# A two-block transformer kernel: column groups in the compressed products, the last steps by row tile, and three reorderings

## What is computed

```python
def compress_kv(kv, pe, w1, b1, w2):        # 15 windows of 32 rows, stride 16, for 2 groups
    blocks = kv[:, idx] + pe[None, None, :, None, :]
    flat = blocks.transpose(0, 1, 3, 2, 4).reshape(B, n_cmp, G, CMP_BLOCK * dk)
    hid = jax.nn.gelu(flat @ w1 + b1)       # a sum over 32 positions of 128 x 128 products
    return hid @ w2
...
    o_cmp = jnp.einsum('bghqn,bngd->bqghd', p.astype(v_cmp.dtype), v_cmp)
    o = gc[..., 0:1] * o_cmp + gc[..., 1:2] * o_slc + gc[..., 2:3] * o_win
...
    x = x + rms_norm(u @ w_down[l], norm_mlp_post[l])     # the end of the program
```

## Time and profile before

| | us |
|---|---|
| median of 3 runs | 2525.02 |
| the profiled execution | 2525.11 |
| its span | 2523.3 |
| PE busy (matmuls) | 2499.6, 99% of the span |
| PEld busy (weight loads) | 2111.9 |
| DVE busy | 1519.8 |
| ACT busy | 1223.3 |
| POOL busy | 47.9 |

### The profile page before, as it was taken

One profiled execution on the slowest core, in us unless ns is written; L12 is line 12 of the kernel. 1 busy time (PEld: TensorE's weight loads), 2 busy tenths in 40 slices (PEclk: granted clock), 3 DMA queues, 4 the chain that ended last, 5 costly groups with the idle time before them and its releaser, 6 DMA issues.

```text
span 2523.3 us, 32700 instructions
## 1 busy us (share of the span) xinstructions
PE 2499.6 (99%) x12440; PEld 2111.9 (84%) x12440; DVE 1519.8 (60%) x1766; ACT 1223.3 (48%) x1555; POOL 47.9 (2%) x67
## 2 busy tenths in 40 slices
PE   9999999999999999999999999999999999999998
PEld 7888888888888888888887887788788888888886
DVE  5656655655776567746764347655665565564565
ACT  6444556545655355534554444445544443443443
POOL 0101100000000000000000000000000000000000
PEclk9999999999999999999999999999999999999999
DMA  8665455655655555555557455555466556565663
GB/s 318 198 192 173 161 167 164 229 184 167 203 193 190 194 190 184 195 189 194 188 184 241 135 184 164 159 167 183 150 202 192 191 186 198 188 195 188 193 204 117
DMA packets 253216, 472.48 MB, mean 187 GB/s; under 512 B 23296, under 2 KB 28928, under 8 KB 252464
## 3 DMA queue, kind: packets, MB, share of 16 engines
q1 hardware_dynamic: 253104, 470.95, 57.3%
HBM read 468.78 MB, written 2.13 MB: 187 GB/s over the span
## 4 chain that ended last, share of the span: by engine, by line
PE 98%; DVE 1%; issue 1%; ACT 0%; DMA 0%; POOL 0%; POOLq 0%; SPq 0%; DVEq 0%; ACTq 0%
PE psum L1793 22%; PE psum L1759 20%; PE psum L1761 20%; PE psum L1760 19%; PE psum L1798 12%; PE psum L1894 1%; PE psum L1879 1%; PE psum L1820 1%; PE psum L2064 1%; PE psum L1864 1%; PE psum L1854 0%; DVE x_rows L1627 0%; PE psum L2153 0%; PE psum L2016 0%; PE psum L2141 0%
## 5 line engine op out<-in xcount | busy, mean ns | idle before, releaser
L1156 DVE TENSOR_TENSOR wl<-raw,wh 128x1024 fp32r<-128x1024 f32 x855 | 1048.0, 1227 | 930.0 <-ACT wh L713 924.9
L713 ACT ACTIVATE wh<-raw 128x1024 fp32r<-128x1024 f32 x855 | 904.7, 1060 | 1018.1 <-PE psum L1761 607.1
L1759 PE MATMUL psum<-wh,ha 128*128 128x512 f32 x1728 | 692.5, 401 | 0.4 <-DVE ha L1198 0.4
L1761 PE MATMUL psum<-wh,ha 128*128 128x512 f32 x1728 | 674.5, 390 | 0.0
L1760 PE MATMUL psum<-wl,ha 128*128 128x512 f32 x1728 | 672.8, 389 | 0.0
L1761 PEld LDWEIGHTS psum<-wh,ha 128*128 128x128 f32 x1728 | 324.3, 188 | 69.7
L1759 PEld LDWEIGHTS psum<-wh,ha 128*128 128x128 f32 x1728 | 324.7, 188 | 65.8 <-issue 0.8
L1760 PEld LDWEIGHTS psum<-wl,ha 128*128 128x128 f32 x1728 | 325.0, 188 | 65.1
L1793 PE MATMUL psum<-ha,wh 128*128 128x512 f32 x1408 | 336.6, 391 | 0.0
L1793 PEld LDWEIGHTS psum<-ha,wh 128*128 128x128 f32 x1408 | 258.7, 188 | 50.0
L1793 PE MATMUL psum<-hb,wh 128*128 128x512 f32 x1024 | 246.5, 392 | 0.0
(11 more groups left out here) (227 smaller groups left out, 1235.2 us busy)
## 6 DMA issues: line engine op xcount, KB each, us to landing
raw<-in_w_up SPq DMA_DIRECT2D x152, 1024.0 KB, 5.1
raw<-in_w_in SPq DMA_DIRECT2D x116, 1024.0 KB, 5.1
raw<-in_w_down SPq DMA_DIRECT2D x108, 1024.0 KB, 5.0
raw<-in_w_out SPq DMA_DIRECT2D x32, 1024.0 KB, 4.9
raw<-in_w_branch_a SPq DMA_DIRECT2D x8, 1024.0 KB, 4.9
raw<-in_w_branch_b SPq DMA_DIRECT2D x8, 1024.0 KB, 5.0
raw<-in_w_in SPq DMA_DIRECT2D x7, 512.0 KB, 8.3
x_t<-in_x_t SPq DMA_DIRECT2D x8, 256.0 KB, 7.7
```

Source lines behind the costliest of these rows:

```text
L713: act.activation(wh[q % SPLIT_SLOTS][:], raw[q // 2 % RAW_SLOTS][:, 2 * (q % 2):2 * (q % 2) + 2, :], ACT.Copy).then_inc(hi_done, 1)
L1156: dve.tensor_tensor(wl[q % SPLIT_SLOTS][:], raw[q // 2 % RAW_SLOTS][:, 2 * (q % 2):2 * (q % 2) + 2, :], wh[q % SPLIT_SLOTS][:].bitcast(F32 ...
L1759: pe.matmul(acc, hi, wh[s][:, c, :], start=first and c == 0, stop=False)
L1761: ins = pe.matmul(acc, lo, wh[s][:, c, :], start=False, stop=last and c == 1)
```

## The change

- Compressed products: each l goes to one of four groups of 32 PSUM partitions (l modulo 4), with 32 stationary columns (two of them zero), all 32 products of a kv in one piece after steps 15 and 17. The four partial sums are copied as 128 partitions, and the transposes after step 20 become products with `fold`, four stacked identities, which add them up. DVE builds fold and the zero columns at step 11.
- cmp_v and cmp_pt get 128 partitions; POOL zeroes them, and L1891 takes all 128.
- In the last block, steps 4 to 7 are done for row tile 0 first and then for tile 1. Sum, squares, mean, root, additions and output go by tile, with a root for each.
- The memset of warm comes ahead of the wait for par; par's DMA comes first.
- In the retention loop the division of the probabilities (j = 3) comes ahead of the split on DVE; the wait for rtab_in moves to the first rotation; the second pair of plain_lo goes from j == 5 to 4.

```diff
+CMP_M = 32
+CMP_GROUPS = P // CMP_M
-    cmp_in = at("cmp_in", [P, 2, CMP_BLOCK, 2, NCMP], 198)
+    cmp_in = at("cmp_in", [P, 2, CMP_BLOCK, CMP_M], 198)
-    cmp_v = at("cmp_v", [NCMP, 2, HD], 188)
+    cmp_v = at("cmp_v", [P, 2, HD], 188)
-    cmp_pt = at("cmp_pt", [NCMP, 8, SEQ], 180)
+    cmp_pt = at("cmp_pt", [P, 8, SEQ], 180)
...
# SP
+        sp.dma_start(par[:, 0:Q_BQ], a["params"][:, 0:Q_BQ]).then_inc(sem["par_in"], 16)
         x_piece(0)
         sp.dma_start(raw[0][:, 0, :], w_in[:, 0, 0:COLS]).then_inc(sem["raw_k0"], 16)
-        sp.dma_start(par[:, 0:Q_BQ], a["params"][:, 0:Q_BQ]).then_inc(sem["par_in"], 16)
...
+        sp.wait_ge(sem["post_ok"], 8 + 3)
+        sp.dma_start(o[:, 0, 0:3 * COLS], x_rows[:, 0, 0:3 * COLS]).then_inc(sem["out_in"], 16)
+        sp.wait_ge(sem["post_ok"], 8 + 4)
+        sp.dma_start(o[:, 0, 3 * COLS:], x_rows[:, 0, 3 * COLS:]).then_inc(sem["out_in"], 16)
+        for c in range(4):
             cols = slice(c * COLS, (c + 1) * COLS)
+            sp.wait_ge(sem["post_ok"], 12 + c + 1)
+            sp.dma_start(o[:, 1, cols], x_rows[:, 1, cols]).then_inc(sem["out_in"], 16)
# POOL
+        pool.wait_ge(sem["gate_ok"], 1)
+        pool.memset(cmp_v[:], 0.0).then_inc(sem["cmp_clear"], 1)
+        pool.wait_ge(sem["cin_ok"], 2)
+        pool.wait_ge(sem["cs_mm"], 1)
+        pool.memset(cmp_pt[:], 0.0).then_inc(sem["cmp_clear"], 1)
...
-        late_root(5, 2)
+        late_root(5, 2, (0,))
+        late_root(5, 3, (1,))
# DVE
+        dve.memset(warm[:], 0.0).then_inc(sem["warm_set"], 1)
         dve.wait_ge(sem["par_in"], 16)
...
+            if s == 11:
+                by = ident[:].rearrange("p (g m) -> p g m", g=CMP_GROUPS)
+                chain.link(dve.tensor_tensor(fold[:], by[:, 0, :], by[:, 1, :], ALU.add))
+                for g in range(2, CMP_GROUPS):
+                    chain.link(dve.tensor_tensor(fold[:], fold[:], by[:, g, :], ALU.add))
+                dve.memset(cmp_in[:, :, :, 2 * NCMP:CMP_M], 0.0)
...
-        dve.wait_ge(sem["rtab_in"], 48)
         for s in range(8 * RET_BLOCKS):
+            scaled = s < RET_START and s % SLOT == 2
+            if scaled:
+                head_stage(3, N1 + s // SLOT, NH)
             ahead(S_RET + s)
-            if s < RET_START:
+            if s < RET_START and not scaled:
                 head_stage(1 + s % SLOT, N1 + s // SLOT, NH)
             if s in rotations:
+                if rotations[s] == (0, 0):
+                    dve.wait_ge(sem["rtab_in"], 48)
...
-            if j in (2, 5):
-                for f in range(2 * (j == 5), 2 * (j == 5) + 2):
+            if j in (2, 4):
+                for f in range(2 * (j == 4), 2 * (j == 4) + 2):
...
+        last_columns(0)
+        tile_mean_square(0)
+        dve.wait_ge(sem["norm_rs"], 6)
+        for c in range(3):
+            add_normed(5, slice(c * COLS, (c + 1) * COLS), (0,))
+        last_columns(1)
+        add_last(0)
+        tile_mean_square(1)
+        dve.wait_ge(sem["norm_rs"], 7)
+        for c in range(3):
+            add_normed(5, slice(c * COLS, (c + 1) * COLS), (1,))
+        add_last(1)
# TensorE
+        def tile_by_tile(q0, src, g, ready):
+            for t in range(NT):
+                acc = psum[:, row_bank(g) + t, :]
+                for j in range(4, 8):
+                    if t == 0:
+                        ready(j)
+                        pe.wait_ge(lo_done, q0 + j + 1)
...
+                if t == 0:
+                    ins.then_inc(sem["first_tile"], 1)
...
-            if 15 <= s < 19:
-                kv, part_ = divmod(s - 15, 2)
+            if s in (15, 17):
+                kv = (s - 15) // 2
...
+                for l in range(CMP_BLOCK):
+                    m0 = CMP_M * (l % CMP_GROUPS)
+                    ins = pe.matmul(psum[m0:m0 + CMP_M, 4 + kv, 0:HD], cmp_in[:, kv, l, :], w1[:, kv, l, :],
+                                    start=l < CMP_GROUPS, stop=l >= CMP_BLOCK - CMP_GROUPS)
+                ins.then_inc(sem["hid_mm"], 1)
...
-                    ins = pe.transpose(psum[:, 7, 2 * NCMP * kv:2 * NCMP * (kv + 1)], hid_t[:, kv, :],
-                                       ident[0:2 * NCMP, 0:2 * NCMP])
+                    ins = pe.matmul(psum[:, 7, CMP_M * kv:CMP_M * (kv + 1)], hid_t[:, kv, :], fold[:],
+                                    start=True, stop=True)
```

More of the change, by code:

```diff
@@ L322, in build @@
     pairs = at("pairs", [P, NT, 2], small + 3.8125)
+    fold = at("fold", [P, CMP_M], small + 3.84375)
     warm = at("warm", [P, SEQ], 198)
@@ L1002, in _ @@
                 act.wait_ge(sem["hid_mm"], kv + 1)
-                act.activation(hid_t[:, kv, :], psum[0:2 * NCMP, 4 + kv, 0:HD], ACT.Copy
+                act.activation(hid_t[:, kv, :], psum[:, 4 + kv, 0:HD], ACT.Copy
                                ).then_inc(sem["hid_copied"], 1)
@@ L1036, in _ @@
             if s == 38:
+                act.wait_ge(sem["cmp_clear"], 2)
                 for f in range(4):
                     act.wait_ge(sem["cpt_mm"], f + 1)
-                    act.activation(cmp_pt[:, 2 * f:2 * f + 2, :], pair(4 + (f + 1) % 4, rows=NCMP), ACT.Copy
+                    act.activation(cmp_pt[0:NCMP, 2 * f:2 * f + 2, :], pair(4 + (f + 1) % 4, rows=NCMP), ACT.Copy
                                    ).then_inc(sem["cpt_ok"], 1)
@@ L1301, in input_lo @@
             ins.then_inc(sem["xt_lo"], 1)
-        dve.memset(warm[:], 0.0).then_inc(sem["warm_set"], 1)
         input_lo(0)
@@ L1739, in _, with tile_mean_square, add_last @@
+        def tile_mean_square(t):
+            dve.wait_ge(sem["norm_ss"], 8 * 5 + 6 + t + 1)
+            r = rstd[:, 10 + t:11 + t]
+            chain.link(dve.reduce_sum(sums[:, 10 + t:11 + t], part[:, 5, t, :], AX.X))
+            dve.tensor_scalar(r, sums[:, 10 + t:11 + t], 1.0 / D, EPS, ALU.mult, ALU.add
+                              ).then_inc(sem["var_ok"], 1)
+        def add_last(t):
+            dve.wait_ge(sem["last_gained"], t + 1)
             dve.scalar_tensor_tensor(x_rows[:, t, last], last_gained[:, t, :], rstd[:, 10 + t:11 + t],
@@ L1762, in rows_step @@
             ins.then_inc(mm_done, 1)
+        def tile_by_tile(q0, src, g, ready):
[5 more added lines that the diff above has]
+                        pe.wait_ge(lo_done, q0 + j + 1)
+                    s = (q0 + j) % SPLIT_SLOTS
+                    for c in range(2):
+                        hi, lo = (src[:, 2 * j + c, part, t * P:(t + 1) * P] for part in range(2))
+                        pe.matmul(acc, hi, wh[s][:, c, :], start=False, stop=False)
+                        pe.matmul(acc, hi, wl[s][:, c, :], start=False, stop=False)
+                        ins = pe.matmul(acc, lo, wh[s][:, c, :], start=False, stop=j == 7 and c == 1)
+                    if t:
+                        ins.then_inc(mm_done, 1)
+                if t == 0:
+                    ins.then_inc(sem["first_tile"], 1)
         def row_blocks(step0, g0, n, per, src, ready=None, extra=None):
@@ L2213, in _ @@
                     pe.wait_ge(chan_free, FREE + C_UP2[p] + 4)
-                for j in range(8):
+                ends = g == R_DOWN2[-1] + 3
+                for j in range(4 if ends else 8):
                     hb_by(11 + 4 * p, 4)(j)
                     rows_step(S_DOWN2[p] + 8 * b + j, 0, 0, ha, (2 * j, 2 * j + 1), g, j == 0, j == 7)
+                if ends:
+                    tile_by_tile(S_DOWN2[p] + 8 * b, ha, g, hb_by(11 + 4 * p, 4))
             rows_before = R_DOWN2[p] + 4
```

73 lines of the change are left out of this document (26 added, 47 removed).

## The result

The changed kernel takes 2504.15 us in the median of 4 runs (2502.84 to 2506.27), the kernel before 2525.09 beside it on the same chip (4 runs, 2524.77 to 2525.94): ratio 0.9913, 95% interval 0.9901 to 0.9924. Its profiled run took 2506.27, its span is 2504.5; the span before was 2523.3, so the two traces are 18.9 apart (unrounded 2523.32 and 2504.47).

The account below looks back on a forecast made before the run. The prediction took TensorE's stream, with its few holes, head and tail, as the bound (98% of the chain). Terms 6.6 + 3.1 + 2.1 + 0.6 + 0.5 + 3.1 = 16.0 took 2525.1 to 2509.1 us, range 2505 to 2516.

Parts of the forecast that it names:

- Part 1: Compressed products (L2064) in four column groups: 64 products at 0.121 us, 7.8 instead of 14.0; with batches 6.6 gained.
- rival C: Compressed products: all four column groups abreast, both records; 10.5 + 0.4 gained, 2504.8 us; chance 0.10.
- The upper bound: Compressed products: four abreast cut streaming from 14.0 to 3.5 us, 10.5 gained.
- below 2506, order within pairs is not what I think: Sign for the compressed products: a total time below 2506 us would refute the assumed order within record pairs.
- A: Compressed products: no overlap of column groups, fp32 record pairs serialise; gain only 0.4, 2515.3 us; chance 0.18.
- B: Compressed products: each weight load waits for the stream in flight; 35 us more, 2550 us; chance 0.04.
- D: Padding doesn't remove the switches or the tail stays serial: 3 us less gain, 2512.1 us; chance 0.06.
- Part 2: Zero padding of cmp_v and cmp_pt (L1891): no switch, 0.39 us a head, 3.1 gained; bounds 1.5 to 5.5.
- Part 3: Retention projection: scaling probabilities ahead of DVE's split removes three PE waits; 2.1 us gained, nothing late next.
- Part 4: Second plain_lo pair at j == 4 instead of 5: PEld's 0.8 us wait for ha goes; 0.6 gained.
- Part 5: Start, earlier warm memset and par: step 1 near 12.4 instead of 13.01; 0.5 us gained, bounds 0.6 lost to 0.6 gained.
- Part 6: Last steps by row tile: tile 0's tail runs beside tile 1's products; 3.1 us gained, bounds 2 to 4.

Follow-up runs that it names:

- g_one: Changed kernel with all compressed products in the first column group instead of four; ran once, 2516.75 us, a batch costs 7.31.
- g_blocks: Changed kernel with eight consecutive compressed products to one column group before the next group's turn; ran once, 2512.21 us, a batch costs 6.09.
- pad_off: Changed kernel with the slc output products (L1891) taking 15 rows again instead of 128; ran once, 2507.67 us.
- tail_off: Changed kernel with the last steps and tail as before, both row tiles complete with the last product, one root; ran once, 2507.37 us.
- pad_64: Changed kernel with the slc output products (L1891) taking 64 rows instead of 128; ran once, 2506.19 us.
- scale_off: Changed kernel with the probabilities scaled behind the weight split again in the retention projection; ran once, 2506.54 us.
- the repeat: Second profile of the unaltered changed kernel, taken in the run after_again; 21.2 us below the span before.
- fill: Changed kernel plus five extra warm-up products between step 0 and step 1; median 2504.84 us.
- start_off: Changed kernel with the old start: memset of warm behind the wait for par, par loaded in its old place; median 2508.01 us.
- groups_only: Kernel before plus only the column-group edits of the compressed products (CMP_M, fold, hid_t, two batches); median 2515.19 us, ratio 0.9952.
- after_again: The changed kernel unaltered, run once more on another chip as standard; median 2503.84 us.
- fill_split: Changed kernel plus five extra warm-up products behind step 0 and the 32 products of 15 columns in two lots; median 2502.77 us.
- fill_split_again: fill_split run once more, unaltered, as standard for the last runs; median 2502.66 us.
- fill_more: fill_split plus twelve products of 128 columns in TensorE's wait for x_rows; median 2501.96 us, ratio to before 0.9902.

## Why the prediction was right and wrong

**Part 1, wrong step.** "If starts stay in program order, only the second record of one group and the first of the next run together" put a product at 0.109 + 0.012. The runs show four records of four groups in 0.11, so 64 products cost 3.5, not 7.8: 10.9 gained instead of 6.6, rival C, which I gave 0.10. I had worked out its 10.5 + 0.4 and set it aside by "a product's own two records and program order"; the first holds (g_one) and binds nothing, as three other groups fill the wait, the second is false (g_blocks). The upper bound was the right value, and the sign that I had named for it ("below 2506, order within pairs is not what I think") came.

The Trainium skill (TensorE: Matmul & The Clock Gate, Part 3) gives that order as strict; g_blocks disagrees for fp32. Its 2.38 is for three column groups, which no run here has; from one to four groups it is 7.31/2.09 = 3.5 here with entry and exit, and by the fit above three would give some 2.7 (an estimate).

**Rivals A and B** fell with the same rows. B's exposed loads: 64 loads of 110 ns fill 1.69 us, so they run abreast too. Neither half of D came true (pad_off, tail_off).

The Trainium skill (same part) lets a load overlap matmuls only where the row group differs. By that, B; the rows above speak against it.

**Part 2, right.** 0.39 a head, 3.1, and 0.03 more a head in the step behind, together 3.4. I had only inferred that full rows remove the switch; pad_off and pad_64 show it. The Trainium skill (TensorEngine Tiling, Key Properties) ties the drain to a change of tiling mode, and 64 rows is such a mode; the trace agrees, 0.39 for the way in and out.

**Part 3, right** (2.1, scale_off), and nothing was late next. **Part 4**: 0.64 at its place in the stream for a forecast of 0.6; it wasn't undone alone. Both forecasts were the middle between PE's wait and PEld's, taken without a reason for the middle: that they fit to 0.1 is partly luck, the waits that go were rightly named.

**Part 5, wrong in size, and a term that wasn't there.** "its weights land just ahead of 10.05" took one landing for the rule. ACT's rounding of step 1's weights starts anywhere from 8.28 to 10.05 in these traces, and in the old order step 1 can't use an early landing, since step 0 stands before it (step 2 at 15.31 to 16.79 in four traces). In the new order it can: 13.81 to 14.70 in eight traces without half clock. Against that, I named the idle TensorE as a bound ("0.6 lost (mirror; TensorE now idles between warm-up and step 1)") without seeing its price: in two of ten traces of the new start the clock fell behind it and step 2 came at 16.29 and 16.37. These are the two with the longest waits, step 1's first product 2.6 and 2.8 behind step 0's last; 2.35 (pad_64) did nothing.

The stretch of half clock at 1440 was in no term at all: 1.6 lost in both profiles of the changed kernel, gone with two lots.

**Part 6, mis-sized.** Forecast 6.1 for DVE's part behind PE, measured 5.80: the front part is 2.5 instead of 2.3, the root with its hand-over 0.6 instead of 1.1, the additions 2.7 as forecast. The term carried the old root's 1.06 over to a root by tile, which takes 0.55. The output's 0.64 I had kept for the bound; why it is shorter ("less traffic ahead of the last output") wasn't tested. 3.43 + 0.64 = 4.1, just above my upper bound of 4.

**The sum.** In the repeat's trace the errors are +4.3 (part 1), +0.3 (part 2), +1.0 (part 6), +1.0 (start), +0.2 (x_rows) and -1.6 (clock at 1440): 5.2, its 21.2 less the 16.0 of the forecast. The median's gain is off by 4.9. In the first trace the start is 1.2 below its term instead, which hides part of the miss, as the clock does in both. The range failed because it "ends just above C" and let no other term be better beside it: C with the tail's upper bound alone is 2503.9.

## What to carry to other kernels

The streaming of small fp32 products with 32 or fewer output rows shrank in proportion to the column groups used: spread them over all four and sum the groups with one small product. Pad a product of few input rows between full ones to 128 rows. Where TensorE waits, or runs many products of few columns in one lot, read the granted clock behind it before comparing two kernels by their spans; a few dummy products in the wait, or two lots for one, cost next to nothing. And line up the same products of both traces instead of adding waits.

## What the hardware showed that I had not expected

- Records of different column groups run four abreast and out of program order, 0.007 us between starts: batches of 7.31, 3.82, 2.09 us for 1, 2, 4 groups.
- 64 rows cost the same switch as 15: 0.39 us in and out, and 0.03 in the step behind.
- Half clock came behind waits of TensorE of 2.2, 2.4 and 3.7 us, and behind 3.6 us of products of 15 columns although TensorE was 100% busy there. Waits of 2.0 (pad_64) and less did nothing. Thirteen traces here have those 32 products in one lot: in ten the clock fell, behind them or (fill, start_off, tail_off) among the last of them; in three it didn't (before, groups_only, pad_64). In two lots: in none of five. The products are the same in all thirteen, and why three escaped isn't settled.
- Covering the places steadied the time: four runs of after_again lie 2.6 us apart, of fill_split 0.3 and of fill_split_again 0.9, of fill_more 0.2. The kernel before, with none covered, ran between 2524.0 and 2529.6 beside the last of these. All its runs above 2526.5 have a mean granted clock of 0.996, all below 2525.7 one of 0.997 or 0.998: it too seems to have such stretches by chance, so the -1.6 of the table, measured against a trace of it without one at 1440, can't be read as a loss that only the changed kernel has.
